# First weight piece of six stages split in halves, and the merge's input copied back half by half

## The reference

```python
h  = modulate_2(rms_norm_2(x, g_norm1[i]), sh1, sc1)
hc = modulate_2(rms_norm_2(ctx, g_norm1[i]), mc[0], mc[1])
p  = h @ w_in[i]
pc = hc @ w_in[i][:, :(N_CTX_COLS if last else N_IN_COLS)]
...
y = g[..., 0, :] * (y_na @ na_w_o) + g[..., 1, :] * (y_gm @ gm_w_o) + g[..., 2, :] * (y_mla @ mla_w_o)
mix = y @ w_out
x_new = x + gt1 * mix
x_new = x_new + gt2 * squared_relu_mlp(modulate_2(rms_norm_2(x_new, g_norm2[i]), sh2, sc2), ffn_w1[i], ffn_w2[i])
```

## Time and profile before

| | |
|---|---|
| median of 3 runs | 3980.21 us (3978.87 to 3986.53) |
| the profiled execution's own time | 3981.97 us |
| its span, first to last instruction | 3980.2 us |
| TensorE matmuls busy | 3421.7 us, 86% |
| VectorE, ScalarE, GpSimd busy | 1562.5, 1108.8, 651.7 us |
| TensorE's share of the chain that ended last | 59% |
| granted TensorE clock, mean | 0.925 |

### The profile page before, as it was taken

How to read it: one execution, slowest core, us unless ns; L and a number is a source line. 1 busy time by engine, 2 the same in 40 slices (tenths; PEclk the granted TensorE clock), 3 DMA queues, 4 the chain that set the end, 5 groups by cost and what they waited for, 6 DMA issues and landing times.

```text
span 3980.2 us, 41148 instructions
## 1 busy us (share of the span) xinstructions
PE 3421.7 (86%) x16083; PEld 2357.8 (59%) x16083; DVE 1562.5 (39%) x2666; ACT 1108.8 (28%) x1931; POOL 651.7 (16%) x475
## 2 busy tenths in 40 slices
PE   4999784888764989788999799999599798988998
PEld 2666642222223865446885588888485456847886
DVE  3336531000014645552432433333474553424444
ACT  3113410121113235443221322221234443313221
POOL 1000001000003334123220100000345124400000
PEclk8999795889987999899999899999799999999999
DMA  6883032999986110002112212111621002233222
GB/s 260 335 317 132 2 147 71 427 428 429 428 344 197 60 35 11 8 35 72 64 53 106 85 64 64 64 64 43 187 71 34 9 35 103 85 126 107 96 94 76
DMA packets 159784, 534.00 MB, mean 134 GB/s; under 512 B 9532, under 2 KB 64724, under 8 KB 136572
## 3 DMA queue, kind: packets, MB, share of 16 engines
q1 hardware_dynamic: 136252, 401.04, 27.1%
q0 software_dynamic: 16880, 92.26, 6.7%
q10 hardware_dynamic: 6480, 38.34, 2.5%
HBM read 488.84 MB, written 42.78 MB: 134 GB/s over the span
## 4 chain that ended last, share of the span: by engine, by line
PE 59%; DVE 5%; ACT 2%; DVEq 1%; DMA 1%; issue 1%; POOL 1%; ACTq 0%; POOLq 0%
PE ps L2810 11%; PE ps L2816 11%; PE ps L1876 7%; PE ps L1878 7%; PE ps L1877 7%; PE ps L514 5%; PE ps L2089 4%; PE ps L2141 2%; PE ps L2129 2%; PE ps L2123 1%; DVE small L2229 1%; DVE Z L2713 1%; DMA ring<-in_w_out_dram 1%; DVEq L222 1%; DVE hT_hi L2717 0%
## 5 line engine op out<-in xcount | busy, mean ns | idle before, releaser
L2810 PE MATMUL ps<-hT_hi,w_hi 128*128 128x512 f32 (+1 forms) x768 | 275.3, 358 | 27.9 <-DVE w_lo L2864 27.9
L2810 PE MATMUL ps<-hT_lo,w_hi 128*128 128x512 f32 (+1 forms) x768 | 276.2, 360 | 0.0
L2810 PE MATMUL ps<-hT_hi,w_lo 128*128 128x512 f32 (+1 forms) x768 | 276.1, 360 | 0.0
L1876 PE MATMUL ps<-wp_hi,hT_hi 128*128 128x512 f32 (+2 forms) x608 | 222.5, 366 | 37.4 <-POOL wp_lo L1855 37.4
L2816 PE MATMUL ps<-w_hi,h_hi 128*128 128x512 f32 x640 | 253.7, 396 | 0.0
L2816 PE MATMUL ps<-w_hi,h_lo 128*128 128x512 f32 x640 | 253.7, 396 | 0.0
L2816 PE MATMUL ps<-w_lo,h_hi 128*128 128x512 f32 x640 | 253.6, 396 | 0.0
L2089 PE MATMUL ps<-Z 64*128 64x256 f32 (+3 forms) x576 | 200.5, 544 | 29.8 <-DVE small L2231 13.1
L2529 POOL TENSOR_TENSOR mr_lo<-ring,wm_hi 128x2048 fp32r<-128x2048 f32 x36 | 170.5, 4747 | 312.4 <-ACT wm_hi L2521 312.2
L1878 PE MATMUL ps<-wp_hi,hm_lo 128*128 128x512 f32 (+2 forms) x608 | 220.7, 363 | 0.0
L1877 PE MATMUL ps<-wp_lo,hT_hi 128*128 128x512 f32 (+2 forms) x608 | 220.1, 362 | 0.0
(11 more groups left out here) (450 smaller groups left out, 6504.1 us busy)
## 6 DMA issues: line engine op xcount, KB each, us to landing
pj<-in_expert_w_up_dram SPq DMA_DIRECT2D x32, 2048.0 KB, 18.3
pj<-in_expert_w_down_dram SPq DMA_DIRECT2D x32, 2048.0 KB, 19.7
ring<-in_expert_w_gate_dram SPq DMA_DIRECT2D x32, 2048.0 KB, 16.0
ring<-in_ffn_w_dram SPq DMA_DIRECT2D x64, 1024.0 KB, 5.2
ring<-in_w_in_dram SPq DMA_DIRECT2D x58, 1024.0 KB, 5.3
Z<-in_w_mod_dram POOLq DMA_DIRECT2D x24, 2048.0 KB, 8.1
Z<-in_w_ada_dram POOLq DMA_DIRECT2D x8, 2048.0 KB, 9.8
ring<-in_w_out_dram SPq DMA_DIRECT2D x6, 2048.0 KB, 16.1
```

The lines of the kernel that those rows point to most:

```text
L1876: nc.tensor.matmul(out_, a_hi, b_hi, start=first, stop=False)
L2810: last = nc.tensor.matmul(bank(i % 8, c1 - c0), W[a][:, k, :], r[:, k, c0:c1], start=(k == 0 and r is hhk and a == 0), stop=(k == KT - 1 a ...
```

## The change

The first piece (x = 0) of each of the six rounded stages is treated by new helpers. ScalarE writes its high part in two instructions of 1024 columns in place of one of 2048, and VectorE subtracts each half as it comes, in the projection and the merge too. GpSimd's loops begin with piece 1. TensorE waits for the first half before the first k of its first tile and for the second half at the middle k. `w_lo_ok` counts one less per stage, so all its values move by one; SP's load that waited for it after piece 0 waits for the second half.

In the merge the reload of hT has a semaphore for each DMA. ScalarE rounds the first half of the weight, waits for the first reload only, copies its half of hT, and rounds the second half of the weight. VectorE makes both low halves, then waits for both reloads and copies its half. TensorE waits for ScalarE's copy before piece 0 and for VectorE's before piece 1.

```diff
+        FIRST = {"proj": 0, "merge": 2, "ffn": 4}
+        def first_piece(stage, l, half):
+            return 6 * l + FIRST[stage] + half + 1
+        def round_first(act, hi, w, half):
+            c = slice(w // 2 * half, w // 2 * half + w // 2)
+            act.activation(hi[:, c], raw[0][:, c], ACT.Copy).then_inc(first_hi_ok, 1)
+        def low_first(dve, stage, l, lo, hi, w, half):
+            c = slice(w // 2 * half, w // 2 * half + w // 2)
+            dve.wait_ge(first_hi_ok, first_piece(stage, l, half))
+            nc.vector.tensor_tensor(lo[:, c], raw[0][:, c], hi[:, c], ALU.subtract).then_inc(first_lo_ok, 1)
...
# sp_proj
-                if x >= 2:
-                    sp.wait_ge(w_lo_ok, R.fp + x - 1)
+                if x == 2:
+                    sp.wait_ge(first_lo_ok, first_piece("proj", l, 1))
+                if x > 2:
+                    sp.wait_ge(w_lo_ok, R.fp + x - 2)
# pool_proj (pool_merge likewise)
-            for x in range(len(R.pieces)):
+            for x in range(1, len(R.pieces)):
# pe_proj (pe_merge and pe_ffn likewise)
-                pe.wait_ge(w_lo_ok, R.fp + x + 1)
+                if x:
+                    pe.wait_ge(w_lo_ok, R.fp + x)
...
+                        if x == 0 and t == ts[0] and k in (0, k1 // 2):
+                            pe.wait_ge(first_lo_ok, first_piece("proj", l, k != 0))
# act_project
-            proj_round(act, n, l, R, 0)
+            act.wait_ge(proj_in[0], 16 * (len(R.pieces) // 2 * l + 1))
+            for half in range(2):
+                round_first(act, WP[0][0], proj_width(l, R, 0), half)
# dve_project, ahead of all else (dve_ffn likewise)
+            for half in range(2):
+                low_first(dve, "proj", l, WP[0][1], WP[0][0], proj_width(l, Proj(dict(n), l), 0), half)
# pe_merge, turn j
+                    pe.wait_ge(hh_back[0], l + 1)
...
+                if j == 0:
+                    pe.wait_ge(hh_back[1], l + 1)
# act_merge
-            act.wait_ge(unspill, 32 * (l + 1))
+            act.wait_ge(mring_in[0], mring_value(l, 0))
+            round_first(act, wm_hi, 2048, 0)
+            act.wait_ge(unspill[0], 16 * (l + 1))
             act.activation(hT_hi[:, 0:3072], hT[:, 0:3072], ACT.Copy).then_inc(hh_back[0], 1)
-            merge_round(act, p, l, 0, 0)
+            round_first(act, wm_hi, 2048, 1)
             merge_round(act, p, l, 0, 1)
# dve_merge
-            dve.wait_ge(unspill, 32 * (l + 1))
+            for half in range(2):
+                low_first(dve, "merge", l, mr_lo, wm_hi, 2048, half)
+            for s in unspill:
+                dve.wait_ge(s, 16 * (l + 1))
             nc.vector.tensor_copy(hT_hi[:, 3072:6144], hT[:, 3072:6144]).then_inc(hh_back[1], 1)
# pe_layer, ahead of pe_merge
-            for s in hh_back:
-                pe.wait_ge(s, l + 1)
```

More of the change, by code:

```diff
@@ L185, in program @@
         wr_ok = sem("wr_ok")
+        first_hi_ok, first_lo_ok = sem("first_piece_hi_ok"), sem("first_piece_lo_ok")
         proj_in = [sem("proj_slot0_in"), sem("proj_slot1_in")]
@@ L1811, in __init__ @@
                     i += len(ts)
-                n["fp"], n["hu"] = self.fp + len(self.pieces), halves
+                n["fp"], n["hu"] = self.fp + len(self.pieces) - 1, halves
         def sp_proj(sp, n, l, rel, f0):
@@ L2525, in pool_merge @@
             merge_counts(n, l)
-            for x in range(18):
+            for x in range(1, 18):
                 n["wr"] += 1
@@ L2538, in half @@
                     kk = 4 * y + k
+                    if j == 0 and y == 0 and t == 0 and k in (0, 2):
+                        pe.wait_ge(first_lo_ok, first_piece("merge", l, k // 2))
                     last = three(bank(b), hhk[:, kk, P * t:P * t + P], hmk[:, kk, P * t:P * t + P],
@@ L2543, in pe_merge @@
             for j in range(6):
-                pe.wait_ge(w_lo_ok, p.fp + 3 * j + 1)
+                if j:
+                    pe.wait_ge(w_lo_ok, p.fp + 3 * j)
+                else:
+                    pe.wait_ge(hh_back[0], l + 1)
                 for t in TQ[l]:
@@ L2772, in __init__ @@
                 self.plan = Plan(n, "-" * i)
-                n["fr"], n["fo"], n["fh"], n["fp"] = self.base["fr"] + h, self.base["fo"] + i - h, self.base["fh"] + h, self.base["fp"] + len(self.pieces)
+                n["fr"], n["fo"], n["fh"], n["fp"] = self.base["fr"] + h, self.base["fo"] + i - h, self.base["fh"] + h, self.base["fp"] + len(self.pieces) - 1
             def last(self, x):
@@ L2780, in sp_ffn @@
             for x, (kind, hb, half, _) in enumerate(F.pieces):
-                if x >= 4:
-                    sp.wait_ge(w_lo_ok, F.base["fp"] + x - 3)
+                if x == 4:
+                    sp.wait_ge(first_lo_ok, first_piece("ffn", l, 1))
+                elif x > 4:
+                    sp.wait_ge(w_lo_ok, F.base["fp"] + x - 4)
                 elif rel[x // 2]:
@@ L2795, in pe_ffn @@
             for x, (kind, hb, half, groups) in enumerate(F.pieces):
-                pe.wait_ge(w_lo_ok, F.base["fp"] + x + 1)
+                if x:
+                    pe.wait_ge(w_lo_ok, F.base["fp"] + x)
                 if kind == "y":
@@ L2808, in pe_ffn @@
                         for k in range(KT):
+                            if x == 0 and i == groups[0][0] and k in (0, KT // 2):
+                                pe.wait_ge(first_lo_ok, first_piece("ffn", l, k != 0))
                             for a, r in ((0, hhk), (0, hlk), (1, hhk)):
@@ L2833, in split @@
                 act.activation(WHI[x % 2], raw[x % 4], ACT.Copy).then_inc(w_hi_ok, 1)
-            split(0)
+            act.wait_ge(raw_in[0], raw_slot_value(l, 0))
+            for half in range(2):
+                round_first(act, WHI[0], 2048, half)
             split(1)
@@ L2862, in split @@
                     return
-                dve.wait_ge(w_hi_ok, len(F.pieces) * l + x + 1)
+                dve.wait_ge(w_hi_ok, (len(F.pieces) - 1) * l + x)
                 nc.vector.tensor_tensor(WLO[x % 2], raw[x % 4], WHI[x % 2], ALU.subtract).then_inc(w_lo_ok, 1)
-            split(0)
+            for half in range(2):
+                low_first(dve, "ffn", l, WLO[0], WHI[0], 2048, half)
             split(1)
```

12 lines of the change are left out of this document (6 added, 6 removed).

## The result

| | before | changed |
|---|---|---|
| median of 5 runs | 3980.21 us (3977.36 to 3986.53) | 3949.03 us (3946.95 to 3958.13) |
| ratio of the runs | | 0.9923, 95% interval 0.9907 to 0.9938 |
| span of the profiled execution | 3980.2 us | 3950.0 us |
| its granted clock, mean | 0.925 | 0.929 |

The change takes 31.2 us off the median and 30.2 off the profiled span; forecast were 30.4. The page's groups at the starts first: busy, mean ns, then idle before and its releaser (they answer to the earlier trace rows).

What follows compares the result with a forecast made beforehand. The prediction took the rounded stages to be bound, beyond their matmuls, by the time from fence to TensorE's first matmul. Six terms sum to 30.4 us off the median 3980.21, giving 3949.8, range 3943 to 3958.

Steps and rivals of the forecast that it cites:

- The starts: Start to first matmul: 2.52 us in projection and FFN from ScalarE's start, 3.86 in the merge from its release.
- Layer 0's projection, 2.7: Layer 0's projection starts 4.18 us earlier but keeps 2.7, since 1.5 becomes a wait on GpSimd at piece 2.
- rival A: Layer 0's projection: piece 2's landing follows its earlier issue, so 31.9 us off in all, 3948.3; chance 0.12.
- Layer 1's projection, 4.2: Layer 1's projection keeps 4.2 us: piece 2 is ready at 2873.6, wanted at 2876.4, so no stop.
- The merges, 9.8 and 9.9: Merge starts come 9.8 us earlier in layer 0, 9.9 in layer 1, from the order and the split wait.
- The FFNs, 1.9 each: Each FFN's ScalarE start to first matmul falls from 4.45 to 2.52 us, 1.9 gained in both layers.
- the clock I cost at nothing: All six starts: the clock's rise may move a microsecond either way, worth half that, about 1 us over six.
- The sum: Six stages: 2.7 + 4.2 + 9.8 + 9.9 + 1.9 + 1.9 = 30.4 us off the span.
- B: Projections: VectorE's second half meets GpSimd's piece 1, both projections gain nothing; 23.5 us off, 3956.7; chance 0.08.
- C: Merges: clock still up at the start, 2 to 3 us more gained, 3947.5; chance 0.1.
- D: Merges start on something later (weight, first reload or second reload), each losing 3.3 us, 3956.4; chance 0.05.
- E: All six starts: TensorE, stopped within its first tile, stays long at clock 0.50; slower than before, 4010; chance 0.02.

Runs made afterwards that it cites:

- e4: Changed kernel with the first piece uncut: ScalarE rounds and VectorE subtracts it whole in all six starts; 3959.13 us, ratio 0.9951 to the kernel before.
- e3: Kernel before with only the merge's new order and split reload wait, no halves, GpSimd still subtracting; 3960.50 us, ratio 0.9960.
- e5: Changed kernel, but ScalarE waits for both reloads before copying its half of hT in the merge; 3959.99 us, one run.
- e8: Changed kernel with the merge's first hT copy shared between VectorE (k 0 and 1) and ScalarE (k 2 and 3); 3948.95 us, one run.
- e7: Changed kernel with the projection's table write issued behind the load of piece 2, GpSimd's table work later; 3950.02 us, one run.
- e1: Kernel before with the merge's part of the change alone, projection and FFN as before; 3956.22 us, ratio 0.9944.
- e10: The changed kernel run once more, beside the kernel before on the same chip; 3949.11 us, ratio 0.9925 to the kernel before.
- e2: Kernel before with the projection's and FFN's part of the change alone, merge as before; 3968.48 us, ratio 0.9978.
- e6: Changed kernel with ScalarE's projection order turned to first half, piece 1, second half, so GpSimd starts before VectorE's second half; 3951.14 us, one run.

## Why the prediction was right, point by point

**The starts.** Worked out 2.52 us for projection and FFN, 3.86 for the merge; measured 2.53 and 3.92 in all runs. The two prices from elsewhere in the trace (1.06 and 1.22 for 1024 columns) held to 0.01. The variants came out by them too: 4.45 and 4.76 where 4.44 and 4.7 stood (e4), 6.82 where 6.7 (e3), 7.42 and 7.20 where 7.2 (e5), 2.57 where 2.52 (e8).

**Layer 0's projection, 2.7.** 2.81 measured, with the stop on GpSimd at 1.49 where 1.5 stood. That it is the table write ahead in the queue is shown by e7; that the landing doesn't follow the issue, by the row of the changed kernel: rival A is out. Over the other traces it is the same: piece 2 is ready 39.9 to 40.9 us after ScalarE's start with the old start (before, e1, e3) and 40.1 to 41.0 in the five with the new one. But the step took the stop for a fixed 1.5. It is 1.1 to 3.4, by when the piece is ready (the write takes 33.7 to 35.5 us from issue to release in this layer) and by how many slow matmuls the start had, and in the two runs where it was 2.43 and 3.38 it cost the clock too. So that 2.81 came out where 2.7 stood is in part luck: over these five traces (changed, e10, e2, e5, e8) the stage took 207.8, 208.5, 210.5, 207.9 and 211.7 us, on average 1.3 below the 210.6 of before.

**Layer 1's projection, 4.2.** 5.04 measured, with two slow matmuls fewer (0.4) and the rest within what untouched stages scatter; 4.0 in e2. "No stop" held here, but by less than the 2.8 us worked out: piece 2 was ready 35.65 us after ScalarE's start before and 36.7 to 38.4 in the traces with the new start, and in e2 and e5, the two latest, TensorE stopped 0.7 and 0.6 us for it.

**The merges, 9.8 and 9.9.** 9.79 and 10.46; in e1 9.57 and 10.12. The step's own remark, that the gain comes from the order and the split wait, was right for most of it: 6.9 by e3's starts; halves and VectorE add 2.9, of which the engine alone has 2.1 (start 6.82 to 4.76, e3 to e4) and the cut 0.8.

**The FFNs, 1.9 each.** Here the term was over-sized in effect: 0.89 and 0.84. The starts gained 1.92; the step "the clock I cost at nothing" failed there, for the traced executions of before and after differ by 5 and 4 slow matmuls, 0.2 us each, against the change. I took the clock's scatter for half a microsecond per start, over six starts about 1 us. Over all traces a start that no stop interrupts has between 7 and 15, some 1.6 us from end to end. It fell against the FFNs and for layer 1's projection; in sum over the six stages (69 slow before, 74 after) it is 1 us, as said. Yet for the FFNs it may not be scatter alone: the eight FFN starts at 4.45 us had 9.8 slow matmuls on average, the sixteen at 2.53 had 12.2, half a microsecond more. Why is not shown.

**The sum.** 29.8 in the six stages against 30.4. Means over all traces whose stage is as before or as changed tell the terms from their scatter:

```
                     before (traces)  changed (traces)  gain  worked out
layer 0 projection        210.6 (3)         209.3 (5)    1.3         2.7
        merge             317.4 (2)         307.2 (5)   10.2         9.8
        FFN               547.4 (3)         546.4 (8)    1.0         1.9
layer 1 projection        171.5 (3)         167.0 (5)    4.5         4.2
        merge             217.5 (2)         207.0 (5)   10.4         9.9
        FFN               378.0 (3)         376.5 (8)    1.5         1.9
```

Together 28.9. The mechanisms hold in all six; layer 0's projection and the FFNs were sized too high, the merges a little too low, and these errors partly cancel. The medians' 31.2 carries luck: parts that no edit touches ran 0.4 shorter in the pair of traces and move by several microseconds between runs.

**The rivals.** A out (above). B did not happen, by 0.4 us of order where 0.3 was worked out; e6 shows that it would have cost 3.2 us of stop in each layer and the clock beside it. C did not happen in this trace: granted clock 0.50 from the first matmul in the merges, where the fall came 1.9 and 1.8 us before it. It was a near thing. TensorE is idle 4.41 us before each such merge, in ten merges over five traces, and in four of them (e1 and e10 once, e6 twice) the clock was still at 1.00 at the first matmul and fell 0.3 to 0.8 us after it, with 9 slow matmuls where the other six have 11 to 13. So what C would have given is 0.6 us and not 2 to 3: the clock fell while TensorE was at work again. D did not happen; e5 prices its place. E did not happen, since no start is stopped within its tile, but half of its mechanism is real: e6 shows that a stop there puts off the rise of the clock.

## What to carry to other kernels

Time the start of a stage link by link, from the fence to the first matmul, and ask of each link whether the first tile needs all of it: the reload for later columns, the second half of a weight, the slower engine. Here such a sum of links held to 0.1 us at the changed kernel's six starts and to 0.2 in its variants. What to distrust is what follows the start: the next load, which stands in a queue whose order the gain doesn't change, and the clock, whose scatter here is as large as the smaller terms. Put a bulk write that no one needs soon behind the load that TensorE needs next.

## What the runs showed of the hardware that I had not expected

A short stop of TensorE in full work costs its length, or some 1.7 times its length where the clock falls for it: behind stops of up to 1.91 us no matmul ran at the low clock, behind 2.43 us 8 did (1.6 us more) and behind 3.38 us 13 (2.5 us more). That is one stop of each length, so where the line runs between 1.9 and 2.4 us, and whether it is a line, is not shown. The clock can also fall after TensorE has taken up its work again, as behind the stop of 2.43 us and in four merges 0.3 to 0.8 us behind their first matmul. And a stop right after a cold start wastes what was done before it: six slow matmuls, a stop of 3.2 us, then eleven to thirteen slow matmuls more (e6, both layers), within the 7 to 15 of a fresh start.

The untouched attention stages of the same code took 344.9 to 351.1 us in layer 0 and 277.7 to 283.4 in layer 1 over the traces. What sets them in one execution was not tried.
